# A decoder block on eight cores: norms in pieces, loads behind the x tiles, transposes ahead of the modulation, the attention output scaled later

## The reference, cut to what matters

```python
mod = silu(c) @ w_ada + b_ada                 # shift1, scale1, gate1, shift2, scale2, gate2
h = rmsnorm(x, norm1_w) * (1 + scale1) + shift1
q, k, v, g, lr, cb, cc, cx, ga, gb = split(h @ w_in)
log_a = log_sigmoid(lr @ w_gate_up + b_gate) / 16
o = gated linear attention(q, k, v, log_a)    # 4 heads, S_t = diag(a_t) S_{t-1} + k_t^T v_t, o_t = q_t S_t
y_a = (rmsnorm(o, gla_norm_w) * silu(g)) @ w_proj_a
y_b = (cb * causal_conv3(cc * cx, conv_w)) @ w_proj_b
x = x + gate1 * ((sigmoid(ga) * y_a + sigmoid(gb) * y_b) @ w_out)
h2 = rmsnorm(x, norm2_w) * (1 + scale2) + shift2
x = x + gate2 * (relu(h2 @ w_mlp1)**2 @ w_mlp2)
out = rmsnorm(x, final_norm_w)
```

## Time and profile before

| | us |
|---|---|
| median of 3 runs | 1482.77 (1481.08 to 1648.66) |
| the profiled execution | 1481.43 |
| its span, slowest core (7) | 1479.8 (cores 1477.7 to 1479.8) |
| mean granted TensorE clock | 0.944 to 0.945 on all cores |
| TensorE, VectorE, ScalarE busy | 89%, 52%, 32% of the span |

### The profile page before, as it was taken

One profiled execution on the slowest core, in us unless ns is written; L12 is line 12 of the kernel. 1 busy time (PEld: TensorE's weight loads), 2 busy tenths in 40 slices (PEclk: granted clock), 3 DMA queues, 4 the chain that ended last, 5 costly groups with the idle time before them and its releaser, 6 DMA issues.

```text
span 1479.8 us, 19267 instructions; the slowest of 8 cores (1477.7 to 1479.8 us)
## 1 busy us (share of the span) xinstructions
PE 1315.2 (89%) x6796; PEld 629.0 (43%) x6796; DVE 762.7 (52%) x1225; ACT 472.9 (32%) x1028; POOL 34.1 (2%) x69
## 2 busy tenths in 40 slices
PE   0599978879997999999999999659999999999992
PEld 0244454435444444444444444324444444444440
DVE  1366732656656555543222234544665665665675
ACT  2455632665533222232111112345112112112332
POOL 2000000000000000000000000000000000000000
PEclk9689889889998999999999999779999999999996
DMA  9934310100062364541131138003033033031122
GB/s 179 208 93 127 103 58 1 58 1 1 19 110 51 51 100 73 92 80 35 29 54 32 29 55 237 21 1 72 1 58 54 3 58 57 1 57 29 57 85 86
DMA packets 17838, 93.10 MB, mean 63 GB/s; under 512 B 2240, under 2 KB 2240, under 8 KB 11856
## 3 DMA queue, kind: packets, MB, share of 16 engines
q0 software_dynamic: 7632, 52.46, 21.1%
q1 hardware_dynamic: 10112, 39.40, 8.1%
HBM read 135.93 MB, written 8.39 MB: 98 GB/s over the span
## 4 chain that ended last, share of the span: by engine, by line
PE 75%; ACT 9%; DVE 7%; issue 5%; DMA 4%; ACTq 0%; DVEq 0%; SPq 0%
PE psf L266 73%; DMA xb<-x_prev 4%; ACT xn L239 3%; ACT tmp L239 2%; DVE tmp L242 2%; PE psf L276 2%; DVE x L242 1%; ACT on L239 1%; ACT lnv L239 1%; ACT S_bf L239 1%; DVE tmp L254 1%; DVE on L248 0%; DVE S L254 0%; ACT rstd L239 0%; ACT hT L239 0%
## 5 line engine op out<-in xcount | busy, mean ns | idle before, releaser
L266 PE MATMUL psf<-hT,wsl 128*128 128x512 bf16 x2944 | 668.7, 384 | 3.7 <-DVE cbuT L242 2.2
L266 PEld LDWEIGHTS psf<-hT,wsl 128*128 128x128 bf16 x2944 | 289.8, 99 | 352.6 <-issue 23.7
L239 ACT ACTIVATE tmp<-psf 128x512 f32<-128x512 f32 (+1 forms) x272 | 156.9, 585 | 591.2 <-PE psf L266 590.3
L266 PE MATMUL psf<-wsl,aT 128*128 128x512 bf16 x1024 | 223.5, 379 | 0.0
L266 PEld LDWEIGHTS psf<-wsl,aT 128*128 128x128 bf16 x1024 | 100.0, 98 | 121.0 <-issue 0.2
L242 DVE TENSOR_TENSOR aT<-tmp 128x512 bf16<-128x512 f32 x128 | 86.9, 691 | 112.0 <-ACT tmp L239 112.0
L242 DVE TENSOR_TENSOR tmp<-tmp,psf 128x512 f32<-128x512 f32 (+1 forms) x72 | 45.2, 627 | 152.3 <-ACT tmp L239 152.3
L242 DVE TENSOR_TENSOR x<-x,tmp 128x512 f32<-128x512 f32 x160 | 110.8, 693 | 17.7 <-DVE tmp L242 2.8
L242 DVE TENSOR_TENSOR tmp<-psf,g2b 128x512 f32<-128x512 f32 x128 | 88.2, 689 | 24.8 <-PE psf L266 24.8
L266 PE MATMUL psf<-wsl,zT 128*128 128x512 bf16 x256 | 63.7, 415 | 8.1 <-ACT hT L239 8.1
L254 DVE SCALAR_TENSOR_TENSOR tmp<-ub,cst,tmp 128x512 f32<-128x512 f32 x64 | 48.0, 751 | 35.5 <-ACT tmp L239 32.1
(11 more groups left out here) (144 smaller groups left out, 1049.6 us busy)
## 6 DMA issues: line engine op xcount, KB each, us to landing
wsl<-w POOLq DMA_DIRECT2D x16, 1024.0 KB, 10.1
wsl<-w_ada POOLq DMA_DIRECT2D x12, 1024.0 KB, 10.9
xb<-x_prev SPq DMA_DIRECT2D x16, 512.0 KB, 21.0
xb<-x_cur SPq DMA_DIRECT2D x16, 512.0 KB, 5.1
wsl<-w_merge POOLq DMA_DIRECT2D x8, 1024.0 KB, 9.5
x<-x_cur SPq DMA_DIRECT2D x16, 512.0 KB, 10.0
out<-x SPq DMA_DIRECT2D x16, 512.0 KB, 2.6
wsl<-w_conv POOLq DMA_DIRECT2D x8, 768.0 KB, 14.3
```

What stands on the lines that cost most here:

```text
L239: P.op("act", lambda e: e.activation(out=out, in_=in_, func=func, **kw), r, w)
L266: ins = e.matmul(out=o, lhsT=l, rhs=rh, start=st, stop=sp_)
```

## The change

The norm is cut into `sq` (sum of squares of one tile; logarithm and exponential once, for all four, with the last) and `xscale` (the scaling of one tile), which stand as pieces between others; in the passes the squares are written to an unused part of `hT`, later to a temporary. The first transposes go into four banks before the adaLN chunks are multiplied and are evicted after the modulation is there. `xload(1)` waits for the load of the fourth adaLN chunk, the loads that the adaLN chunks used to trigger come one to two per pass and wait until the x tiles just asked for have landed. `xload` stands at the start of a pass or block. `phaseO`'s scalings become `phaseN`, behind the next state update, and `phaseT` moves ahead of it. In the dense blocks the gates come among the last v pieces.

```diff
-        def rec_load(j):
+        def rec_load(j, after=()):
...
-            P.op("pool", lambda e: e.dma_start(out=dst, in_=src), [], [("w", j % NW)], dma=f"w{j % NW}")
+            P.op("pool", lambda e: e.dma_start(out=dst, in_=src), list(after), [("w", j % NW)], dma=f"w{j % NW}")
...
-        def done_w(n=1):
+        def done_w(n=1, after=()):
...
-                    rec_load(j)
+                    rec_load(j, after)
...
-        def xload(i, dst=xb, sub=4):
+        def xload(i, dst=xb, after=()):
...
-                P.op("sp", lambda e, c=c, d=d: e.dma_start(out=dst.t[:, d, :], in_=src[c]), [],
+                P.op("sp", lambda e, c=c, d=d: e.dma_start(out=dst.t[:, d, :], in_=src[c]), list(after),
...
-            done_w()
...
-        def norm(i):
+        def sq(i, s):
+            if i < 6:
+                j_, jk = hT.t[:, 1, 0:2, :].rearrange("p k c -> p (k c)"), hT.k((4096, 1024))
+            else:
+                j_, jk = tmp()
+                j_ = j_[:, :].bitcast(BF16)
+            A(j_, xb.t[:, s, :], AF.Square, xb.k((s * 1024, 1024)), jk + [("ss", s)],
+              accum_out=ss[:, s:s + 1])
+            if s == 3:
+                A(lnv[:, :], ss[:, :], AF.Ln, [("ss", s_) for s_ in range(4)], ["lnv"], scale=1.0 / D, bias=EPS)
+                A(rstd[:, :], lnv[:, :], AF.Exp, ["lnv"], ["rstd"], scale=-0.5)
+        def xscale(i, s):
...
-            for s in range(4):
-                A(xn.t[:, s, :], xb.t[:, s, :], AF.Square, xb.k((s * 1024, 1024)), xn.k((s * 1024, 1024)) + [("ss", s)],
-                  accum_out=ss[:, s:s + 1])
-                A(lnv[:, s:s + 1], ss[:, s:s + 1], AF.Ln, [("ss", s)], [("lnv", s)], scale=1.0 / D, bias=EPS)
-                A(rstd[:, s:s + 1], lnv[:, s:s + 1], AF.Exp, [("lnv", s)], [("rstd", s)], scale=-0.5)
-                Vsmul(xn.t[:, s, :], xb.t[:, s, :], rstd[:, s:s + 1], xb.k((s * 1024, 1024)) + [("rstd", s)],
-                      xn.k((s * 1024, 1024)))
-                if i == 4 and s == 0:
-                    Vsmul(xn32.t[:, :], xb.t[:, 0, :], rstd[:, 0:1], xb.k((0, 1024)) + [("rstd", 0)], xn32.k())
-            if i < 7:
-                xload(i + 1)
+            Vsmul(xn.t[:, s, :], xb.t[:, s, :], rstd[:, s:s + 1], xb.k((s * 1024, 1024)) + ["rstd"],
+                  xn.k((s * 1024, 1024)))
+            if i == 4 and s == 0:
+                Vsmul(xn32.t[:, :], xb.t[:, 0, :], rstd[:, 0:1], xb.k((0, 1024)) + ["rstd"], xn32.k())
+        def sq_piece(i, s):
+            return (0.01, lambda: sq(i, s))
+        def xs_piece(i, s):
+            return (0.01, lambda: xscale(i, s))
...
-        norm(0)
+        for s in range(4):
+            sq(0, s)
+        for s in range(4):
+            xscale(0, s)
+        hold = []
+        for kp in range(4):
+            _, pk, pb = bank()
+            TR([(pb[:, j * 512 + s * 128:j * 512 + (s + 1) * 128], xn_of(0).t[:, s, (kp * 2 + j) * 128:(kp * 2 + j + 1) * 128])
+                for j in range(2) for s in range(4)], xn_of(0).k(), pk)
+            hold.append((pb, pk))
...
+        xload(1, after=[("w", 3)])
...
+        for kc in range(8):
+            pb, pk = hold[kc // 2]
+            o = pb[:, kc % 2 * 512:(kc % 2 + 1) * 512]
+            rd = pk + ["a1T", ("modT", 0), ("modT", 4)]
+            if kc // 2 % 2:
+                Vts(hT.t[:, 2, kc, :], o, a1T[:, kc:kc + 1], modT[:, kc:kc + 1], ALU.mult, ALU.add, rd, hk(2, kc))
+            else:
+                A(hT.t[:, 2, kc, :], o, AF.Identity, rd, hk(2, kc), scale=a1T[:, kc:kc + 1], bias=modT[:, kc:kc + 1])
...
-        run([tr_piece(0, kc, ALLB) for kc in range(8)])
-        norm(1)
...
+        for s in range(4):
+            sq(1, s)
+        for s in range(4):
+            xscale(1, s)
...
-            if i == 2:
-                P.op("sp", lambda e: e.dma_start(out=w32q.t[:, :, :].rearrange("p k c -> p (k c)"), in_=W["q"][0]), [], w32q.k(), dma="c5")
-                P.op("sp", lambda e: e.dma_start(out=w32k.t[:, :, :].rearrange("p k c -> p (k c)"), in_=W["k"][0]), [], w32k.k(), dma="c6")
+            xload(i + 2)
+            if i < 2:
+                done_w(1, xb.k())
+            elif i == 2:
+                done_w(2, xb.k())
+                P.op("sp", lambda e: e.dma_start(out=w32q.t[:, :, :].rearrange("p k c -> p (k c)"), in_=W["q"][0]), xb.k(),
+                     w32q.k(), dma="c5")
+                P.op("sp", lambda e: e.dma_start(out=w32k.t[:, :, :].rearrange("p k c -> p (k c)"), in_=W["k"][0]), xb.k(),
+                     w32k.k(), dma="c6")
...
-            run(ms[0:4])
-            run([lr_piece(i + 1, ALLB)])
-            run(ms[4:6])
-            run(gate_pieces(i + 1, ALLB))
-            run(ms[6:8])
-            norm(i + 2)
+            gs = gate_pieces(i + 1, ALLB)
+            run(ms[0:3] + [lr_piece(i + 1, ALLB)] + ms[3:4])
+            run([sq_piece(i + 2, 0), ms[4], gs[0], gs[1], sq_piece(i + 2, 1), ms[5], gs[2], gs[3], sq_piece(i + 2, 2)])
+            run(ms[6:8] + [sq_piece(i + 2, 3)] + [xs_piece(i + 2, s) for s in range(4)])
...
+                    st[s] = pos
+                return (0.9, f)
+            def phaseN(s):
+                g = t * 4 + s
+                i0 = s * 4
+                def f():
+                    o_ = on[g % 2]
...
-                        po, pok = pos[h // 2]
+                        po, pok = st[s][h // 2]
...
-                return (0.9, f)
+                return (0.01, f)
...
+                if s >= 1:
+                    out.append(phaseT(s - 1))
...
-                if s >= 1:
-                    out.append(phaseT(s - 1))
+                out.append(phaseN(s))
...
-            out = qk + [vs[0], ktr(t % 2, 3, DB), vs[1]]
-            if t < 3:
-                i = t + 5
-                out += [tr_piece(i, 0, DB), tr_piece(i, 1, DB), vs[2], tr_piece(i, 2, DB), tr_piece(i, 3, DB), vs[3],
-                        tr_piece(i, 4, DB), tr_piece(i, 5, DB), vs[4], tr_piece(i, 6, DB), tr_piece(i, 7, DB), vs[5],
-                        vs[6], lr_piece(i, DB), vs[7]]
-                if i < 7:
-                    out.append((0.01, lambda: norm(i + 1)))
-                out += gate_pieces(i, DB)
-            else:
-                out += vs[2:]
+            i = t + 5
+            if t == 3:
+                return qk + [vs[0], ktr(t % 2, 3, DB)] + vs[1:]
+            tr = [tr_piece(i, kc, DB) for kc in range(8)]
+            gs = gate_pieces(i, DB)
+            nx = i < 7
+            out = [(0.01, lambda: xload(i + 1))] if nx else []
+            out += qk + [vs[0], ktr(t % 2, 3, DB), tr[0], tr[1], vs[1], tr[2], tr[3], vs[2], tr[4], tr[5], vs[3], tr[6], tr[7]]
+            out += [sq_piece(i + 1, 0)] if nx else []
+            out += [vs[4]]
+            out += [sq_piece(i + 1, 1)] if nx else []
+            out += [lr_piece(i, DB)]
+            out += [sq_piece(i + 1, 2)] if nx else []
+            out += [vs[5], gs[0]]
+            out += [sq_piece(i + 1, 3)] if nx else []
+            out += [gs[1], vs[6]]
+            out += [xs_piece(i + 1, s) for s in range(2)] if nx else []
+            out += [gs[2], gs[3]]
+            out += [xs_piece(i + 1, s) for s in range(2, 4)] if nx else []
+            out += [vs[7]]
...
+                done_w()
...
```

## The result

The changed kernel takes **1503.14 us** (median of 4 runs, 1499.98 to 1503.73) where the kernel before takes 1482.42 beside it: ratio **1.0138** with the interval [1.0119, 1.0158]. The forecast was 1490 with 1462 to 1508: the sign of its small difference was right, its size (+8 against +21 us) was not. In some executions, such as one of the kernel before that took 1648.66 us, the cores of one die or both are granted a lower clock, and the ratios leave these out. The profiled execution took 1503.19 us, with a span of 1501.5 on its slowest core, core 5.

The account below looks back on a forecast made before the run. TensorE, busy 89% of the span, was taken as the bound. From 1481.4 us: start and passes -10.8, D0 -6.8, D1 +5.8, D2 +9.0, D3 +2.3, C +9.0 gave 1490 us, range 1462 to 1508.

Parts of the forecast that it names:

- Start and passes: Start of the kernel and passes over previous tokens: 10.8 us gained, first q matmul at about 185 us.
- Rival 4: The start doesn't gain: first transposes before the adaLN chunks put 4 us on the path; 1498 us, chance 0.13.
- D0: First of four dense blocks (D0 to D3): squares spread between matmuls remove TensorE's idle, gain 6.8 us (3 to 8).
- The gaps: New TensorE waits for the late scaling in dense blocks D1 to D3 and first convolutions C; 11 new gaps.
- O3 of D1: Wait before the fourth phaseO in the second dense block, behind a gate's scan and the late scaling: 5.5 us.
- T3 of D2: Wait before the last phaseT in the third dense block, for exponential pair, scan and late scaling: 5.0 us.
- O1 of C: Wait before the second phaseO in the first convolutions, behind a convolution piece, state update and scaling: 4.8 us idle.
- T3 of D1: Wait before the last phaseT in the second dense block, with two tile scalings and two scans more in line: 7.6 us.
- the clock term of late scaling: Third dense block's tail from v4 to next phaseA: 25.6 us at full clock, 28.4 at low; 26.8 taken.
- rival 1: Every gap drops the clock: 11 new gaps, each followed by about 3 us lost; 1515 us, chance 0.10.
- Rivals 2 and 3: Late scaling hidden, 1453 us, chance 0.10; only half of the gaps there, 1477 us, chance 0.17.
- The rule against this change: Skill section: a kernel waiting between short matmul bursts runs each burst cold and pays at every wait; priced through 1515 us.

Follow-up runs that it names:

- experiment 9: Changed kernel with the scaling put back in phaseO and the first transposes after the adaLN chunks, as before the change: 1460.52 us, ratio 0.9851.
- experiment 8: Changed kernel with the scaling put back in phaseO and the weight and x tile loads not held back: 1465.44 and 1466.44 us, ratio 0.9887.
- experiment 6: Kernel before with the changed start and passes alone; norm in the first two dense blocks one block of squares and scalings: 1478.02 us, ratio 0.9964.
- experiment 4: Changed kernel with 57 unread matmuls half filling its eight longest TensorE waits: 1498.53 us, ratio 1.0099.
- experiment 10: Changed kernel with scaling back in phaseO, first transposes after the modulation, and each block's last phaseT in a bank of its own: 1447.28 us, ratio 0.9749.

## Why the prediction was right in part and wrong in its size

- **Start and passes (-10.8): exact.** Transposes of group 1 at 70.64 (70.3 forecast), a pass 27.6 us long (27.9), first q matmul at 184.99 (185). The working behind it holds for ScalarE's order. It did not price the order of the transposes by itself: it took the change's order as given, while the old order gains 5 us more (experiment 9). The held loads, priced at nothing, are worth nothing (experiment 8). Rival 4 named the right mechanism, matmuls put on the path, but it costs 5 us out of a larger gain and does not undo the gain.
- **D0 (-6.8): -6.0.** Right, and experiment 6 shows that this needs the spread squares: without them D0 lost 2.9.
- **The gaps: right in place and nearly in length.** O3 of D1 5.5 forecast and 4.44 measured, O3 of D2 4.4 and 3.74, T3 of D2 5.0 and 4.53, O1 of C 4.8 and 5.68, the next phaseA in C 2.4 and 2.60, O3 of C 3.9 and 3.66. Only T3 of D1 was over-sized, 7.6 against 4.53: the two tile scalings expected in line ahead of it were already done. That all idle comes to 22.0 us against 22.6 is in part luck: by the gap list, O3 and T3 of D1 and D2 were to be 13.1 and 9.4 us and measured 9.0 and 8.3.
- **The failed step: the clock term of late scaling.** The sum had "28.4 at the low one behind each gap; I take 26.8" for D2's tail and nothing for D1 and C, 1.2 us; rival 1 called what the sum held "about 4". Busy time rose by 5.0, 4.5 and 5.0 us in D1, D2 and C, 14.5 us, and filling the gaps gives 13.7 back. Nearly the whole miss, 21 against 8 us, is this term. The tails from v4 to the next phaseA show it closest: 29.5 us forecast for D1 and 26.8 for D2, 32.3 measured in both. Less the two gaps of each, the forecast leaves 16.4 and 17.4 us for the matmuls; in the kernel before they took 18.0, and now they take 23.3 and 24.1. Even the 28.4 us "at the low one behind each gap" falls short. The error was to take the low level as 3 us behind single gaps, and for D2 less than that. In D1 the two long gaps stand 17 us apart, and every row between them is at the low level; so it is in D2 on the profiled core, while on five others part of these rows is at the full level, and D2 is 2 us shorter. In C there are five waits within 50 us, and the stretch was at 0.85 on the whole. There the phaseA that "stays where it is" came 4.8 us later in the stretch (38.9 us after its start, not 34.1): 1.3 us more idle and 3.5 us more busy time.
- **Rival 1**, every gap drops the clock, was half right. Eight waits of 3.66 us and more were seen on the profiled core; behind seven of them the next row is at the low level, and behind the eighth (3.66) the first matmuls are still at the full one and the 24 that follow take 7.03 us, where 24 take 5.34 elsewhere in C. Most of the short ones did not drop the clock: behind 0.97 and 1.50 us in D1 and 1.61 and 1.73 in D3 a `v,scb` matmul takes 0.27 us and not 0.37, and behind 2.60 in C phaseA takes 0.38. D3 ran at 0.98, with +2.5 us as forecast. But length is not the rule: experiment 4 has the low level behind 1.94 us, experiment 10 behind 1.17 and 0.82, and so has D2 of the kernel before, in a row that the prediction did not look at:

```profile
379.20 1.01 PE L276 MATMUL psf<-ident,on 128*128 128x128 bf16 x8 [1.10 <-DVE ogT L257]
```

In these three places the short wait stands close behind gate matmuls (16 rows, float32), which is not so for those that left the clock alone in D1 and D3. That the gates are the reason was not tried. The prediction's reading "the 2.28 us row speaks against, 2.85 for" goes by length alone, and the rows do not bear that out.
- **Rivals 2 and 3** fell: no gap was hidden. D2 was 66.1 us and not 54.
- **The rule against this change.** The Trainium skill, "TensorE: Matmul & The Clock Gate", section "HAM oscillation — how this bites in real kernels", has short bursts of matmuls between waits that are longer than the bursts run cold, every one of them. It would have given the right sign of the error, and between the long gaps of D1 the rows here agree with it, although the 12 us of work between them is no short burst: 3.59 us for a projection of 1.89. Short waits are not the case of that section; here they went both ways (rival 1).
- **The 2% bounds** 1453.1 and 1511.1 us were reckoned from two different times, 1482.8 and 1481.4; no conclusion hangs on it.

Shown by runs: that late scaling loses 37 us in this frame, and 27 in the old one together with the earlier `phaseT`; that 13.7 of the 37 come back when the gaps are filled, at a higher granted clock; that bank 0 behind VectorE's queue costs 13 us by the times, 10.5 by the stretches; that the first transposes' place costs 5. Not shown: how D0's gain divides between its idle and its clock, and what besides a wait's length decides whether the clock falls behind it. A late scaling that reads banks of its own was not tried.

## What to carry to other kernels

Before an eviction is moved behind other work, ask who reuses its bank: TensorE waits for it through everything that stands ahead on the evicting engine, and it was cheaper to evict at once, or to give the next user another bank. Price the gap and the matmuls between this gap and the next one as two terms: here they were 22 and 14.5 us, and the second is read from the busy time of a window with equal counts. Where the first data comes later than the weights, let the matmuls that need only weights go first. Do not read from the length of a wait alone whether the clock falls behind it; read the durations of the rows that follow, on more than one core.

## What the runs showed that was not expected

- Work put into waits shortened the kernel: 120 unread matmuls in eight gaps took the granted clock from 0.94 to 0.96 and the time from 1503.14 to 1489.46 us; 57 of them gave 4.6 us, 3.2 of them in D1 and next to nothing in D2.
- The waits cost 1.7 times their length: idle grew by 22.0 us and the same matmuls by 14.5.
- The rows behind a wait of 1.10 us were at the low level at once (D2 of the kernel before); behind one of 3.75 us (O3 of D2 in the kernel after) five of eight cores began at the full level, and the low one came with the gates 1.7 us later.
- Removing a wait uncovered one of the same length with another releaser: T3 of D1 4.53 us on `on` in the kernel after, 4.58 on `ogT` without late scaling, none with a bank of its own.
